# Order of the first rows, the sample gate, the last stores and the keys at the borders of three stages

## What is computed

```python
z = rms_norm(x, g_mix) @ w_in                  # 1024 -> q 512, k 512, v 512, f 8, a 512, gate 512
logf = log_sigmoid(f + b_f)
attn = fox_attention(q, k, v, logf, k_past, v_past, logf_past)     # 8 heads of 64
u = a * sigmoid(gate)
conv = silu(layer_norm(depthwise_conv31([conv_past, u]) + b_dw))   # 31 taps, 512 channels
x = x + concat(attn, conv) @ w_out
# PEER: 8 heads, 16 of 128*128 experts for each row and head
q = rms_norm(x, g_ffn) @ w_pq
expert, score = top16 of (q . sub_keys), over pairs of half scores
x = x + sum_k softmax(score)_k * gelu(xn . u_emb[expert_k]) * v_emb[expert_k]
y = rms_norm(x, g_final)
```

## Time and profile before

| | us |
|---|---|
| median of 3 runs | 3480.57 (3479.92 to 3481.24) |
| the profiled execution | 3483.33 |
| its span, first to last instruction | 3481.3 |
| stage A, to the first PE instruction of B | 378.9 |
| stage B, to SP's first issue of C | 465.0 |
| stage C | 2837.5 |

### The profile page before, as it was taken

How to read it: one execution, slowest core, us unless ns; L and a number is a source line. 1 busy time by engine, 2 the same in 40 slices (tenths; PEclk the granted TensorE clock), 3 DMA queues, 4 the chain that set the end, 5 groups by cost and what they waited for, 6 DMA issues and landing times. The chain is left out here.

```text
span 3481.3 us, 41296 instructions
## 1 busy us (share of the span) xinstructions
PE 2498.5 (72%) x13379; PEld 1024.4 (29%) x13379; DVE 2490.2 (72%) x6867; ACT 997.5 (29%) x2816; POOL 1476.5 (42%) x1266
## 2 busy tenths in 40 slices
PE   8999789676667667766776677667666766766664
PEld 4444566422222222222222222222222222222221
DVE  4888577677677767767766777677667766767885
ACT  3333344322222222222222222222222222222331
POOL 2333131144444544444444444544444444444543
PEclk9999788788789888888888797878888888888877
DMA  4000100699999999999999999999999999999997
GB/s 156 24 24 25 71 31 19 233 421 421 420 411 419 415 417 415 416 414 422 416 411 420 413 408 419 419 412 418 415 419 414 414 416 418 411 372 421 416 421 321
DMA packets 194556, 1198.42 MB, mean 344 GB/s; under 512 B 31051, under 2 KB 41379, under 8 KB 55102
## 3 DMA queue, kind: packets, MB, share of 16 engines
q0 software_dynamic: 156672, 1140.92, 79.6%
q1 hardware_dynamic: 37694, 55.13, 4.5%
HBM read 1181.14 MB, written 14.84 MB: 344 GB/s over the span
## 5 line engine op out<-in xcount | busy, mean ns | idle before, releaser
L1284 PE MATMUL ps<-uv_rows,diag 64*64 64x512 f32 x8704 | 1366.1, 754 | 886.5 <-ACT diag L1397 880.7
L1194 POOL DMA_INDIRECT uv_rows<-in_uv_emb,experts x1088 | 1307.4, 1202 | 1486.2 <-PE ps L1284 1276.6
L1543 DVE CUSTOM_DVE_ANT_0 uv_rows<-uv_rows,xn_c 128x1024 f32<-128x1024 f32 x1088 | 1333.0, 1226 | 735.6 <-DMA uv_rows<-in_uv_emb,experts 730.2
L1284 PEld LDWEIGHTS ps<-uv_rows,diag 64*64 64x64 f32 x8704 | 326.8, 155 | 1627.3 <-ACT diag L1397 1202.1
L1389 ACT ACTIVATE gelu_c<-dots 128x2 f32<-128x2 f32 x544 | 110.7, 204 | 1751.2 <-DVE dots L1543 1751.0
L1397 ACT ACTIVATE diag<-ident_twice,act_c 128x64 f32<-128x64 f32 x1088 | 319.1, 340 | 286.3 <-DVE act_c L1560 286.1
L1247 PE MATMUL ps<-w_pq_sb,xnT_c 128*128 128x256 f32 x1152 | 345.4, 430 | 0.0
L1247 PEld LDWEIGHTS ps<-w_pq_sb,xnT_c 128*128 128x128 f32 x1152 | 220.3, 208 | 272.8 <-issue 251.4
L571 DVE SCALAR_TENSOR_TENSOR convT<-w_out_sb,tapsT,convT 128x128 f32 x960 | 252.8, 343 | 0.0
L513 PE MATMUL ps<-w_in_sb,w_out_sb 128*128 128x512 f32 (+1 forms) x656 | 240.6, 522 | 11.1 <-ACT w_out_sb L405 11.1
L339 POOL TENSOR_TENSOR rstd_a<-ms_a,neg_half 128x1 f32<-128x1 f32 x9 | 86.9, 9659 | 178.3 <-ACT ms_a L386 178.3
(11 more groups left out here) (208 smaller groups left out, 2124.7 us busy)
## 6 DMA issues: line engine op xcount, KB each, us to landing
uv_rows<-in_uv_emb,experts POOLq DMA_INDIRECT x1088, 12.5
w_in_sb<-in_w_in SPq DMA_DIRECT2D x4, 2048.0 KB, 14.4
w_pq_sb<-in_w_pq SPq DMA_DIRECT2D x8, 1024.0 KB, 12.1
cat_turned<-catT SPq DMA_DIRECT2D x9, 512.0 KB, 2.6
w_out_sb<-in_x_prompt SPq DMA_DIRECT2D x8, 512.0 KB, 3.3
w_out_sb<-in_w_out SPq DMA_DIRECT2D x1, 4096.0 KB, 12.7
catT_c<-cat_turned SPq DMA_DIRECT2D x8, 512.0 KB, 8.3
out<-x_c SPq DMA_DIRECT2D x8, 512.0 KB, 8.3
```

Of the source, the lines that this page charges most:

```text
L1194: nc.gpsimd.indirect_dma_start(out=rows[:, m % RING, :], out_offset=None, in_=d.uv_emb[0], in_offset=bass.IndirectOffsetOnAxis(ap=experts[ ...
L1284: ins = pe.matmul(ps[dst, 2 * x + half, :], diag[src, (m + i) % DIAGS, :], rows[src, (m + i) % RING, cols], start=first, stop=last)
L1543: nc.vector.tensor_tensor_reduce(out=row, in0=row, in1=xn[:, block_of(n) % 2, :], scale=1.0, scalar=0.0, op0=ALU.mult, op1=ALU.add, accum_ ...
```

## The change

- Stage A, set-up: SP issues the gate weights right after the vectors, ahead of taps, state, bias and the past. ACT squares the first rows as soon as they are there, then makes the set-up's copies, then norms the first rows, and copies the past keys out last. POOL makes the first rows' scale before the past keys' column. `logfs` moves into the working space in `w_out_sb`.
- Stage A, end: DVE's loop covers seven blocks; block 7 is written out as straight code, and `gated` of the sample runs in it ahead of tap 23 of 31.
- Stores: stage A's last waits for stores stand in stage B, on SP after the loads of the rows and gains and before that of w_out, which now comes third. Stage B's waits for `cat_turned` stand in stage C, on SP before the first load of it and on POOL before the first gather.
- Stage C: SP loads w_pq's first part ahead of the sub-keys. PE multiplies head 0 first, then turns the keys of heads 0 to 3 (8 transposes), and those of heads 4 to 7 after head 1's multiplication. ACT copies each half out. The eighth gather waits for the second half.

```diff
@@ phase_a, SP
+            load_weights(ORDER[0])
             sp.dma_start(taps[:, :], d.w_dw[0]).then_inc(small_here, 16)
             ...
             sp.dma_start(c.values[:, s.NB, :], d.cache_v[0, 0].rearrange("t h e -> t (h e)")).then_inc(past_here, 16)
-            for name in ORDER:
+            for name in ORDER[1:]:
+                load_weights(name)
@@ phase_a, SP, end
             sp.dma_start(d.logf_sample[0, 0], logfs[0:s.TS, s.NB, :]).then_inc(misc_stored, 16)
-            sp.wait_ge(k_stored, 16 * (1 + BLOCKS))
-            sp.wait_ge(v_stored, 16 * BLOCKS)
-            sp.wait_ge(misc_stored, 80)
@@ phase_a, POOL
-            pool.wait_ge(past_here, 48)
-            pool.wait_ge(cum_ready, 1)
-            nc.gpsimd.tensor_scalar(k_aug[:, :, s.HD], cum_past[:, :], -1.0, None, ALU.mult).then_inc(kaug_ready, 1)
...
             rms_scale(0)
+            pool.wait_ge(past_here, 48)
+            pool.wait_ge(cum_ready, 1)
+            pool.wait_ge(rstd_ready, 1)
+            nc.gpsimd.tensor_scalar(k_aug[:, :, s.HD], cum_past[:, :], -1.0, None, ALU.mult).then_inc(kaug_ready, 1)
@@ phase_a, ACT
-            act.wait_ge(setup_psum, 3)
...
-            act.wait_ge(cum_psum, 1)
-            nc.scalar.copy(cum_past[:, :], ps[:, F_, s.H:2 * s.H]).then_inc(cum_ready, 1)
...
-            keys_out(PAST, s.NB)
...
             row_scale(0)
+            act.wait_ge(setup_psum, 3)
...
+            act.wait_ge(cum_psum, 1)
+            nc.scalar.copy(cum_past[:, :], ps[:, F_, s.H:2 * s.H]).then_inc(cum_ready, 1)
             normed(0)
+            keys_out(PAST, s.NB)
@@ phase_a, DVE
-            def convolved(b, y_of):
+            def convolved(b, y_of, at=None, then=None):
                 dve.wait_ge(uT_ready, b + 2)
                 for j in range(s.TAPS):
+                    if j == at:
+                        then()
...
-            with dve.Fori(0, s.NB) as b:
+            with dve.Fori(0, s.NB - 1) as b:
...
-            nc.vector.tensor_copy(c.uT[:, :, 0:HALO], stateT[:, :, :])
-            dve.wait_ge(misc_stored, 16)
-            gated(s.NB, s.TS, c.uT[:, :, HALO:])
+            def sample_gated():
+                nc.vector.tensor_copy(c.uT[:, :, 0:HALO], stateT[:, :, :])
+                dve.wait_ge(misc_stored, 16)
+                gated(s.NB, s.TS, c.uT[:, :, HALO:], True)
+
+            last = s.NB - 1
+            chain.at(SETUP_LINKS + last * LINKS)
+            gated(last, P, uT[:, :, HALO:HALO + P])
+            convolved(last, lambda i: c.convT[:, i, last * P:s.NB * P], 3 * s.TAPS // 4, sample_gated)
@@ phase_b, SP
-            sp.dma_start(w_out[:, :, :], d.w_out[0].rearrange("(c p) n -> p c n", p=P)).then_inc(w_here, 16)
             sp.dma_start(x1[:, :], d.x_prompt[0, 0:P, :]).then_inc(x_here, 16)
             sp.dma_start(gf[:, :], d.g_ffn[0].partition_broadcast(P)).then_inc(gf_here, 16)
+            sp.wait_ge(c.k_stored, 16 * (1 + BLOCKS))
+            sp.wait_ge(c.v_stored, 16 * BLOCKS)
+            sp.wait_ge(c.misc_stored, 80)
+            sp.dma_start(w_out[:, :, :], d.w_out[0].rearrange("(c p) n -> p c n", p=P)).then_inc(w_here, 16)
...
-            for i in range(2):
-                sp.wait_ge(cat_stored[i], 16 * ((BLOCKS + 1 - i) // 2))
@@ phase_c, SP
             sp.dma_start(xn[:, 0, :], d.xn2[:, :]).then_inc(xn_here, 16)
+            load_queries(0)
...
-            for h in range(PH):
...
+            for h in range(1, PH):
+                load_queries(h)
+            cat_stored(sp)
             load_cat(1)
@@ phase_c, POOL
-                    pool.wait_ge(keys_psum, 1)
+                    pool.wait_ge(keys_psum, 2)
...
+            cat_stored(pool)
@@ phase_c, PE
             turn_rows(0)
+            query(0)
             pe.wait_ge(keys_here, 32)
...
-            query(0)
-            pe.wait_ge(keys_ready, 1)
+            turn_keys(0)
             for r in range(FIRST_ROUTED):
                 turn_query(r)
+                if r == 0:
+                    pe.wait_ge(keys_ready, 1)
                 score(r)
                 query(r + 1)
+                if r == 0:
+                    turn_keys(1)
+            pe.wait_ge(keys_ready, 2)
@@ phase_c, ACT
             rows_out(0)
...
             for r in range(FIRST_ROUTED):
                 query_out(r)
+                if r < 2:
+                    keys_out(r)
                 turned_out(r)
```

More of the change, by code:

```diff
@@ L112, in build @@
         g.ps = ctx.enter_context(nc.psum_tensor("ps", [P, 8, BANK], F32))
+        g.cat_stored = [ctx.enter_context(nc.semaphore(f"cat_stored{i}")) for i in range(2)]
         with ExitStack() as mix:
@@ L136, in caches @@
     c.tapsT = sb("tapsT", [P, s.CCH, s.TAPS])
+    c.k_stored, c.v_stored, c.misc_stored = (ctx.enter_context(nc.semaphore(n)) for n in ("k_stored", "v_stored", "misc_stored"))
     c.g_mix = c.vecT[:, 0:s.DCH]
@@ L261, in _, with load_weights @@
                 sp.dma_start(vecs[lo:lo + s.CCH, :], v[0].rearrange("(c p) -> c p", p=P)).then_inc(small_here, 16)
[L262 to L267 removed]
             w_rows = d.w_in[0].rearrange("(c p) n -> p c n", p=P)
[L269 removed]
+            def load_weights(name):
                 lo, width = COLS[name]
@@ L276, in _ @@
                     sp.dma_start(w_in[:, :, to:to + width], w_rows[:, :, lo:lo + width]).then_inc(w_here[name], 16)
+            load_weights(ORDER[0])
+            sp.dma_start(taps[:, :], d.w_dw[0]).then_inc(small_here, 16)
+            sp.dma_start(state[:, :], d.state_conv[0, 0]).then_inc(small_here, 16)
+            sp.dma_start(bf[:, :], d.b_f[0].partition_broadcast(P)).then_inc(small_here, 16)
+            sp.dma_start(k_aug[:, :, 0:s.HD], d.cache_k[0, 0]).then_inc(past_here, 16)
+            sp.dma_start(logf_past[:, :], d.cache_logf[0, 0]).then_inc(past_here, 16)
+            sp.dma_start(c.values[:, s.NB, :], d.cache_v[0, 0].rearrange("t h e -> t (h e)")).then_inc(past_here, 16)
+            for name in ORDER[1:]:
+                load_weights(name)
             def stores(b, kb, k_out, v_out, rows):
@@ L539, in _, with gated @@
             dve.wait_ge(setup_sb, 3)
-            def gated(b, rows, dst):
+            def gated(b, rows, dst, sample=False):
                 dve.wait_ge(proj_psum, NPROJ * b + 2)
                 dve.wait_ge(sig_ready, b + 1)
-                if isinstance(b, int):
+                if sample:
                     for part, cols in PARTS:
@@ L633, in phase_b @@
             sem("zT_psum"), sem("yn_ready"), sem("held_ready"), sem("gate_ready"), sem("conv_ready"))
-        oT_ready, cat_stored = sem("oT_ready"), [sem(f"cat_stored{i}") for i in range(2)]
+        oT_ready, cat_stored = sem("oT_ready"), g.cat_stored
         x1_psum, x1_ready, ss_ready, rms_ready, xn_ready = (
@@ L1143, in phase_c, with cat_stored @@
         block = ctx.enter_context(nc.Block())
+        def cat_stored(eng):
+            for i in range(2):
+                eng.wait_ge(g.cat_stored[i], 16 * ((BLOCKS + 1 - i) // 2))
         @block.sync
@@ L1309, in gains, with turn_keys @@
                 ins.then_inc(gains_psum, 1)
+            def turn_keys(i):
+                for p in range(2):
+                    for h in range(4 * i, 4 * i + 4):
+                        ins = pe.transpose(ps[:, 2 * p + i, (h % 4) * P:(h % 4 + 1) * P], keys[:, p * PH + h, :], g.ident[:, :])
+                ins.then_inc(keys_psum, 1)
             turn_rows(0)
+            query(0)
             pe.wait_ge(keys_here, 32)
-            for x in range(2 * PH):
-                ins = pe.transpose(ps[:, x // 4, (x % 4) * P:(x % 4 + 1) * P], keys[:, x, :], g.ident[:, :])
-            ins.then_inc(keys_psum, 1)
-            query(0)
-            pe.wait_ge(keys_ready, 1)
+            turn_keys(0)
             for r in range(FIRST_ROUTED):
                 turn_query(r)
+                if r == 0:
+                    pe.wait_ge(keys_ready, 1)
                 score(r)
                 query(r + 1)
+                if r == 0:
+                    turn_keys(1)
+            pe.wait_ge(keys_ready, 2)
             for n in range(HEADS):
@@ L1409, in crossed, with keys_out @@
                 ins.then_inc(crossed_out, 1)
-            rows_out(0)
-            act.wait_ge(keys_psum, 1)
-            for x in range(2 * PH // 4):
-                dst = keysT[:, x // 2, 4 * (x % 2):4 * (x % 2) + 4, :]
-                ins = nc.scalar.copy(dst, ps[:, x, :].rearrange("p (h k) -> p h k", k=s.NKEYS))
-            ins.then_inc(keys_ready, 1)
+            def keys_out(i):
+                act.wait_ge(keys_psum, i + 1)
+                for p in range(2):
+                    ins = nc.scalar.copy(keysT[:, p, 4 * i:4 * i + 4, :], ps[:, 2 * p + i, :].rearrange("p (h k) -> p h k", k=s.NKEYS))
+                ins.then_inc(keys_ready, 1)
+            rows_out(0)
             for r in range(FIRST_ROUTED):
                 query_out(r)
+                if r < 2:
+                    keys_out(r)
                 turned_out(r)
```

25 lines of the change are left out of this document (10 added, 15 removed).

## The result

| | before | changed |
|---|---|---|
| median of 18 runs each, side by side | 3481.57 (3478.49 to 3510.38) | 3470.01 (3464.84 to 3477.29) |
| mean of the same runs | 3489.08 | 3470.94 |
| the profiled execution, its span | 3483.33, 3481.3 | 3473.65, 3471.7 |

What follows compares the result with a forecast made beforehand. Stage C is bound by its transfers, so the lengths of A and B count: 7.9 + 1.3 + 2.1 - 1.4 = 9.9 us off a median of 3480.57 gives 3470.7 us, range 3465.5 to 3476.0.

Steps and rivals of the forecast that it cites:

- A's end: End of stage A: PE's idle hole and slow q projection go, 7.9 us; the barrier's wait goes, 1.3 us.
- The hole and q's slow projection: Sample block in stage A: PE's 6.23 us of idling goes, and q's projection takes 3.67 instead of 5.30 us; together 7.9.
- The covers: End of stage A: logf is ready 1.6 us before PE needs it, and the last taps end 3.2 us before SP's last issue.
- The barrier's wait: Border from A to B: SP no longer waits for the landing of logf, a gain of 1.3 us, bounds 0 and 1.3.
- B's end: Border from B to C: without SP's wait for the last `cat_turned`, C starts 2.1 us earlier, bounds 0 and 2.2.
- A's start: Set-up of stage A: 2.0 us lost up to the first projection, 0.6 won by PE's speed, net loss 1.4 us.
- The delay behind the gate weights: Set-up of stage A: the past lands 5.2 us later, at 14.4, behind 64 packets of gate weights on one DMA engine.
- PE's half speed: First projection instructions of stage A: PE, busy beforehand, may run at full speed, winning 0.6 of the 1.35 us lost.
- one engine works through the 31 rows of taps: Set-up loads: all 31 tap rows sit on one DMA engine, with the other small loads' shares on that engine queued behind.
- C: Start of stage C: the first gather comes perhaps 2 us sooner, worth nothing as transfers bind; length unchanged within 1 us.
- no new wait: Block 0 of stage A: sigmoid and u meet a PE later by 1.4 us, so no new wait arises.

Runs made afterwards that it cites:

- the kernel with this part alone: The kernel before with only block 7's taps as straight code and the sample's gate ahead of tap 23: median 3470.2 us, ratio 0.9979.
- the one with the taps behind the log: The kernel before with one wait added, DVE's second round of taps waiting for POOL's log of the forget gate: mean 3480.3 us, ratio 0.9981.
- these three kernels: The changed kernel with POOL's log operation in block 0 held until 1, 2 or 8 taps are done: medians 3499.2, 3498.0 and 3500.0 us.
- the run with one tap: The changed kernel with POOL's log operation in block 0 held until the first of DVE's 120 taps is done: median 3499.2 us, ratio 1.0037.
- that with the waits alone: The kernel before with only the waits for the last stores of stages A and B moved a stage later: median 3476.7 us, ratio 0.9974.

## Why the prediction was right and wrong

**A's end: right.** The hole and q's slow projection were put at 7.9 us; the kernel with this part alone has 7.7. The covers were as worked out: logf 1.6 us ahead of PE, the last taps ended at 369.1 and SP's last issue at 372.6. The barrier's wait gave 1.1 of 1.3, and B's end 2.1 of 2.1.

**A's start: right in sign, the size too small.** Forecast was a loss of 1.4 us, measured one of 3.7 at block 7, 3.9 by its terms. The chain from the past to the first projection is 6.11 us (6.24 forecast). The delay behind the gate weights was put at 5.2 us and was 5.9 for the small loads and 6.2 for the past. By that mis-sizing the first projection came 0.9 us later than forecast, at 21.50 and not 20.64. The term that came out with the other sign is what the prediction took for PE's half speed: I took 0.6 us of gain because PE would be at work before the projection. It lost 1.1 instead, 5.13 - 6 x 0.44 = 2.5 us over the full pace against 1.35. That slow start is scatter. The run with C's start as before has the same code in stage A, and its PE shows no slow instruction:

```profile
21.91 8.42 PE L517 MATMUL ps<-w_in_sb,w_out_sb 128*128 128x512 f32 x19 [1.34 <-ACT w_out_sb L403]
```

It reached z of block 7 at 323.30 us, 1.9 sooner than the changed kernel's profiled execution, a loss of 1.8 and not 3.7. Over the thirteen profiles none to five of the first projection instructions took 0.86 us instead of 0.43. The granted clock reads 1.00 over all of them in the changed kernel (21.50 to 26.60 us), so no row shows why they are slow. A guess on it should have been put at zero. The reading "one engine works through the 31 rows of taps", on which the 5.2 us stood, is only half supported: a split would then have won 3 us and won 1.

**B: not forecast.** It was 3.7 us shorter, 261.62 to 257.90, with no line of it changed. Windows of 600 to 610 us, of the kernel before and of the one with the taps behind the log, which has the same stage B:

```profile
600.00:610.00 10.00, 10.00 (x57) 7.21 (x56) 6.99 (x16) 3.54 (x6) 1.14 (x2) 0.66 0.13 54
```

```profile
600.00:610.00 10.00, 8.91 (x71) 6.70 (x72) 9.70 (x20) 3.42 (x6) 1.14 (x2) 1.00 0.14 54
```

The same code ran there at a granted clock of 0.66 and of 1.00, and took 261.62 and 258.33 us as a whole. Over the thirteen profiled executions B took 257.0 to 261.6, and 257.0 to 261.3 in those with the changed kernel's own B. I take the 3.7 us for such scatter; it may be where the 2.8 us lay by which the kernel before's profiled execution was over its median, but one trace can't show it.

**C: right.** 2837.4 and 2838.9 us, within the 2832.8 to 2839.1 of all profiled executions; the choice came 1.3 us sooner and was worth nothing that shows.

**The sum of the traces is luck in part.** 9.6 us were measured for a forecast of 9.9, but A's start came out 2.3 worse, C 1.5 worse and B 3.7 better than forecast, and these cancel.

**What failed** is the step in A's start that puts the later PE in block 0 at nothing: the sigmoid and u of block 0 "then meet a PE that is later by 1.4 us, so no new wait". The later PE adds no wait, but it takes one away, which is worth 8.0 us on the mean of the 18 runs (5 of 18 at 28.6 us), and so the difference of the means is 18.1 us and not 9.9. The sum went by one execution, and the three runs shown lay within 1.3 us, so nothing in the times told of a second group. The trace gave a hint: the operation on the log started 0.35 us into the taps in block 0 and 3.9 to 4.0 us ahead of them in every other prompt block, while each scale of POOL's that fell into the taps lasted 12.0 to 12.4 us and not 0.55. In the groups of the kernel before, from 0 to 370 us, it stands out with a mean of 9659 ns for 128 elements:

```profile
L339 POOL TENSOR_TENSOR rstd_a<-ms_a,neg_half 128x1 f32<-128x1 f32 x9 | 86.9, 9659 | 178.3 <-ACT ms_a L386 178.3
```

Those rows show that POOL is held beside the taps, and an operation that comes close to them. Had they been read, the later PE could have been forecast as a gain on the mean: with a quarter of the runs at 29.6 us each, 7.4 us, against its cost of 1.8 to 3.7. The quarter, however, could not be had from three runs. What makes the start late and what ends the long executions is one and the same, the gate weights ahead of the small loads: with these first again and the rest of the change kept, 2 of 12 runs were long.

What stays open is why an operation that comes within the first 0.36 us passes, and others behind it. The share of long executions of one in four is measured and not derived.

## What to carry to other kernels

A trace is one execution: where a kernel's times fall into two groups, look for a small POOL operation that starts within a fraction of a microsecond of a dense DVE run, and for others that last tens of times their usual length, even where that costs nothing. Make such an order certain with a wait on the dense side (here 1.3 us, hidden) rather than leave it to arrival times. When something comes later in a set-up, ask of each pair of chains that were close before which is now first.

## What the runs showed of the hardware that was not expected

- A POOL operation on 128x8 elements that comes behind the first of 120 back-to-back scalar_tensor_tensor steps of 128x128 waits for all of them, if no POOL operation has been let in before it: 31.3, 31.0 and 29.4 us when it came 0.44, 0.69 and 2.27 us after the first one's start, and all 30 runs of these three kernels were long. One that came within 0.36 us passed, and so did those that followed it with gaps of up to 0.59 us. Beside a tensor_scalar of DVE it only grew from 0.26 to at most 0.40 us.
- After the 27.7 us in which PE then stood still, its next eight projection instructions took 6.17 us in the run with one tap, and 5.55 in that with the waits alone, instead of 3.68.
- The issue of the past logf, 4 KB, held SP for 4.43 us with the 2 MB of gate weights issued ahead of it (0.65 us without, 1.96 with the taps split). With the past on ACT's queue, issued before the gate weights, it landed at 5.5 to 6.6 us, and SP's own small loads landed 1.5 us later.
- A barrier of all engines passed with stores in flight: 1.05 us from SP's last issue to B's first PE instruction and 1.23 us from the last `cat_turned` to C's first load, where the waits made it 2.2 and 3.35.
